# Gate and branch projections of a decoder block turned token-major: h and y as the stationary operand, weights moving in 512 columns

## The reference, cut to what matters

```python
h = rms_norm(x, norm_pre_w)
proj = einsum('bsd,df->bsf', h, w_in)
qkv_a, z_a, beta_a, dec_a, qkv_b, z_b, gate_logits = split(proj, cuts)
...                                                  # mixers: ya, yb, each (1, 256, 1024)
gates = sigmoid(gate_logits + b_gate).reshape(bsz, s, 2, d)
pa = einsum('bsf,fd->bsd', ya, w_branch[0])
pb = einsum('bsf,fd->bsd', yb, w_branch[1])
merged = gates[:, :, 0] * pa + gates[:, :, 1] * pb
out = einsum('bsd,de->bse', merged, w_out)
return x + rms_norm(out, norm_post_w)
```

## Time and profile before

| | us |
|---|---|
| median of 3 runs | 367.78 |
| the profiled execution | 368.02 |
| its span in the trace | 366.2 |
| TensorE busy | 356.7 (97%) |
| VectorE busy | 268.8 (73%) |
| ScalarE busy | 219.8 (60%) |
| GpSimd busy | 59.6 (16%) |

### The profile page before, as it was taken

How to read it: one execution, slowest core, us unless ns; L and a number is a source line. 1 busy time by engine, 2 the same in 40 slices (tenths; PEclk the granted TensorE clock), 3 DMA queues, 4 the chain that set the end, 5 groups by cost and what they waited for, 6 DMA issues and landing times.

```text
span 366.2 us, 7651 instructions
## 1 busy us (share of the span) xinstructions
PE 356.7 (97%) x2755; PEld 343.1 (94%) x2755; DVE 268.8 (73%) x559; ACT 219.8 (60%) x500; POOL 59.6 (16%) x119
## 2 busy tenths in 40 slices
PE   7999998999999999999999999999999999999993
PEld 5889997999999999999999999999999999999882
DVE  2869776488986878978788678797885656767644
ACT  4778894454456565767576676766677542433521
POOL 1533441740033001101020202001020100000011
PEclk9999999999999999999999999999999999999998
DMA  8657849789798475445654455554556484874623
GB/s 261 178 179 196 266 124 236 185 221 242 185 225 225 115 194 150 117 117 130 181 146 120 118 143 152 142 140 117 125 153 181 118 223 127 224 230 170 236 110 115
DMA packets 99343, 62.45 MB, mean 171 GB/s; under 512 B 3652, under 2 KB 94190, under 8 KB 99310
## 3 DMA queue, kind: packets, MB, share of 16 engines
q1 hardware_dynamic: 98014, 58.59, 58.2%
q0 software_dynamic: 1296, 3.43, 3.4%
HBM read 60.41 MB, written 1.59 MB: 169 GB/s over the span
## 4 chain that ended last, share of the span: by engine, by line
PE 92%; DVE 2%; ACT 2%; DMA 1%; issue 1%; POOL 0%; DVEq 0%; SPq 0%; ACTq 0%; POOLq 0%
PE banks L1285 67%; PE banks L1499 6%; PE banks L1303 4%; DMA xin<-in_x_dram 1%; PE banks L1382 1%; PE banks L1389 1%; PE banks L1400 1%; PE banks L1270 1%; DVE w_lo L865 1%; PE banks L1438 1%; PE banks L1202 1%; PE banks L1441 1%; DVE acc L939 1%; PE banks L1227 1%; PE banks L1359 0%
## 5 line engine op out<-in xcount | busy, mean ns | idle before, releaser
L865 DVE TENSOR_TENSOR w_lo<-raw,w_hi 128x1024 fp32r<-128x1024 f32 x102 | 124.2, 1220 | 31.3 <-ACT w_hi L634 31.1
L634 ACT CAST w_hi<-raw 128x1024 fp32r<-128x1024 f32 x103 | 106.8, 1046 | 6.0 <-PE banks L1499 2.8
L1285 PE MATMUL banks<-h_hi,w_lo 128*128 128x256 f32 x568 | 82.3, 287 | 0.0
L1285 PE MATMUL banks<-h_lo,w_hi 128*128 128x256 f32 x568 | 82.2, 287 | 0.0
L1285 PE MATMUL banks<-h_hi,w_hi 128*128 128x256 f32 x568 | 82.2, 287 | 0.0
L1285 PEld LDWEIGHTS banks<-h_hi,w_hi 128*128 128x128 f32 x568 | 72.9, 191 | 0.3
L1285 PEld LDWEIGHTS banks<-h_lo,w_hi 128*128 128x128 f32 x568 | 72.7, 191 | 0.0
L1285 PEld LDWEIGHTS banks<-h_hi,w_lo 128*128 128x128 f32 x568 | 72.7, 191 | 0.0
L939 DVE SCALAR_TENSOR_TENSOR acc<-banks,vec,acc 128x255 f32<-128x255 f32 (+2 forms) x72 | 34.5, 479 | 5.9 <-ACT acc L734 3.5
L584 POOL TENSOR_TENSOR so<-so,rnq 128x2 f32<-128x2 f32 x8 | 3.8, 472 | 148.8 <-ACT junk L801 148.8
L845 ACT CAST h_hi<-tacc 128x256 f32 x8 | 3.3, 408 | 28.4 <-DVE tacc L1166 28.4
(11 more groups left out here) (243 smaller groups left out, 544.4 us busy)
## 6 DMA issues: line engine op xcount, KB each, us to landing
raw<-in_w_in_dram SPq DMA_DIRECT2D x80, 512.0 KB, 5.2
raw<-in_w_branch_dram SPq DMA_DIRECT2D x16, 512.0 KB, 4.8
raw<-in_w_out_dram SPq DMA_DIRECT2D x8, 512.0 KB, 4.2
xin<-in_x_dram SPq DMA_DIRECT2D x2, 512.0 KB, 4.0
th_E<-g_rows POOLq DMA_DIRECT2D x2, 512.0 KB, 6.9
bias<-bias_rows POOLq DMA_DIRECT2D x1, 1024.0 KB, 6.5
raw<-in_x_dram SPq DMA_DIRECT2D x2, 512.0 KB, 4.0
out_dram<-xin SPq DMA_DIRECT2D x4, 256.0 KB, 2.0
```

Source lines behind the costliest of these rows:

```text
L634: nc.scalar.copy(w_hi[:, t % SLOTS, :], raw[:, t % SLOTS, :]).then_inc(s_hi, 1)
L865: v.tensor_tensor(w_lo[:, t % SLOTS, cols], raw[:, t % SLOTS, cols], w_hi[:, t % SLOTS, cols].bitcast(F32), ALU.subtract).then_inc(s_lo, 1)
L1285: last = mm(ps, w, r, start=part == 0 and k == 0, stop=part == 2 and k == KT - 1)
```

## The change

- Gates: four tiles now make a group of 512 gate columns for all 256 tokens, in two banks. The loads take 256 rows x 512 columns (pieces of 2 KB; before 1024 rows x 128 columns, pieces of 512 B). A tile is 12 matmuls of 512 columns (`group_third`). Groups 0 to 2 are tiles 16 to 27, group 3 is tiles 76 to 79.
- The gate bias now lies along the free dimension. ScalarE copies each bank to SBUF (two copies of 128x512 per group), GpSimd adds the bias rows (`gate_rows`, two adds of 128x512 per group, both inputs in SBUF), ScalarE takes the tanh of 128x1024 later (S=66, 78, 122). For group 3 VectorE adds from PSUM (`late_gates`, at S=240), with the tanh at S=243.
- The bias rows are broadcast to 128 partitions by DMA: three on SyncE behind the load of tile 12, one on GpSimd ahead of its last `o_norm`. The b_gate load at the start and one VectorE instruction (`vec_half`) are gone.
- On GpSimd `gate_rows(0)` and `(1)` stand behind the bias DMA (L564) and ahead of the wait for the substitution; `gate_rows(2)` stands between the store and the reload of the solved blocks.
- Branches: no loop. Four groups of four tiles: b and a for columns 0 to 511, then b and a for 512 to 1023. VectorE gates them in tiles of 128x512 and adds them to `m_tok`.
- m is now token-major, and w_out needs it channel-major: TensorE turns it (`turn_m`), 8 transposes of 128x128 at S=270 (tile 90) and 8 behind the second tile of w_out. ScalarE and VectorE split it out of PSUM in pieces of 128x512.

```diff
+GATE_TANH = [66, 78, 122, 3 * BRANCH0 + 3]
+M_TURN = 3 * BRANCH0 + 30
...
+        gate_banks = [(bank[0], bank[1]), (bE, bF), (bA, bD), (bC, bD)]
+        m_banks = [(bA, bB), (bank[0], bank[1])]
...
+                if n == 12:
+                    sp.wait_ge(s_bd_p, 1)
+                    for group in range(3):
+                        part = b_gate[512 * group:512 * group + 512].rearrange("(a n) -> a n", a=1)
+                        sp.dma_start(early_rows[group], part.to_broadcast([P, 512])).then_inc(s_rows_e, 16)
...
+            def gate_rows(group):
+
+                pool.wait_ge(s_rows_e, 48)
+                for c in range(NC):
+                    pool.wait_ge(s_gate_raw, 2 * group + c + 1)
+                    pool.tensor_tensor(th[group][:, c, :], th[group][:, c, :], early_rows[group],
+                                       ALU.add).then_inc(s_gate_b, 1)
+
+            gate_rows(0)
+            gate_rows(1)
             pool.wait_ge(s_sub, 2 * STEPS)
             for a in range(2):
                 pool.dma_start(bass.AP(t_blocks.tensor, BLK * a, [[BLK * BLK, HALF], [2 * BLK, BLK // 2], [1, BLK]]),
                                t0[HALF * a:HALF * a + HALF]).then_inc(s_T_out, 16)
+            gate_rows(2)
             pool.wait_ge(s_T_out, 32)
...
+            def gate_front(group, c):
+
+                if c == 0:
+                    sa.wait_ge(s_gate_p, group + 1)
+                else:
+                    sa.wait_ge(s_tile, GATES_A + 4 * group + 4)
+                nc.scalar.copy(th[group][:, c, :], gate_banks[group][c]).then_inc(s_gate_raw, 1)
+
+            def gate_tanh(group):
+
+                sa.wait_ge(s_gate_b, 2 * group + 2)
+                ac(th[group], th[group], ACT.Tanh, scale=0.5).then_inc(s_gate_th, 1)
...
+            def first_branch(half):
+
+                for c in range(NC):
+                    branch_done(half, 1, c)
+                    v.scalar_tensor_tensor(out=th[half][:, c, :], in0=th[half][:, c, :], scalar=1.0, in1=bank[6 + c],
+                                           op0=ALU.add, op1=ALU.mult).then_inc(s_m_a, 1)
+                    ve.wait_ge(s_m_a, 2 * half + c + 1)
+                    ve.wait_ge(s_m_b, 2 * half + c + 1)
+                    v.tensor_tensor(m_tok[c], m_tok[c], th[half][:, c, :], ALU.add).then_inc(s_m_sum, 1)
...
+            def group_third(n, part, left_hi, left_lo, banks, done):
...
+                for kk in range(2):
+                    for c in range(NC):
+                        left = (left_lo if part == 1 else left_hi)[:, 2 * q + kk, P * c:P * c + P]
+                        right = (w_lo if part == 2 else w_hi)[:, slot, 512 * kk:512 * kk + 512]
+                        last = mm(banks[c], left, right, start=q == 0 and kk == 0 and part == 0,
+                                  stop=q == 3 and kk == 1 and part == 2)
...
+            def turn_m(half):
+
+                pe.wait_ge(s_m_sum, 2 * half + 2)
+                if half == 0:
+                    pe.wait_ge(s_gate_b, 8)
+                for k in range(4):
+                    for c in range(NC):
+                        last = tp(m_banks[half][k // 2][:, SEQ * (k % 2) + P * c:SEQ * (k % 2) + P * c + P],
+                                  m_tok[c][:, P * k:P * k + P], ident)
+                last.then_inc(s_m_turned, 1)
```

More of the change, by code:

```diff
@@ L418, in _ @@
             for g in range(EARLY, 2 * KT):
[L419 to L423, removed]
+                gate_load(GATES_B + g - EARLY, g // 4, g % 4)
+            for t in range(2 * KT):
+                half, branch, q = t // 8, 1 - t // 4 % 2, t % 4
+                group_load(BRANCH0 + t, w_branch[branch][256 * q:256 * q + 256, 512 * half:512 * half + 512])
             sp.wait_ge(s_pv_p, HEADS)
@@ L708, in value_front, with m_parts @@
                                ((bE, bF), (bB, bE))[group][c]).then_inc(s_vtok, 1)
[L710 to L717, removed]
+            def gate_front(group, c):
[7 more added lines that the diff above has]
+                ac(th[group], th[group], ACT.Tanh, scale=0.5).then_inc(s_gate_th, 1)
+            def m_parts(half, b):
+                sa.wait_ge(s_m_turned, half + 1)
+                k = 4 * half + 2 * b
+                nc.scalar.copy(m_hi[:, k:k + 2, :], m_banks[half][b].rearrange("p (k n) -> p k n", k=2)).then_inc(s_m_hi, 1)
             def front(h, s):
@@ L809, in stage_w @@
                     nc.scalar.copy(y_hi[:, 0, g:g + 1, :], one(y32[:, 0, :])).then_inc(s_yhi_a, 1)
-            for S in range(3 * BRANCH0):
+            for S in range(3 * OUT0):
                 n, part = S // 3, S % 3
@@ L829, in _ @@
                         front(g, S - A0 - A_STRIDE * g)
[L830 to L833, removed]
+                for group in range(3):
+                    done = 3 * (GATES_A + 4 * group + 4)
+                    if S in (done, done + 1):
+                        gate_front(group, S - done)
+                    if S == GATE_TANH[group]:
+                        gate_tanh(group)
+                if S == GATE_TANH[3]:
+                    gate_tanh(3)
+                if S in (M_TURN + 1, M_TURN + 2):
+                    m_parts(0, S - M_TURN - 1)
                 if part == 1:
                     split_hi(n + LEAD, n + LEAD, (n + LEAD) // SLOTS + 1)
[L836 to L845, removed]
             for k in range(KT - LEAD):
                 split_hi(OUT0 + k + LEAD, k + LEAD, (OUT0 + k + LEAD) // SLOTS + 1)
+                if k == 2:
+                    for b in range(2):
+                        m_parts(1, b)
             for b in range(2 * NC):
@@ L1018, in front @@
                     ve.wait_ge(s_tanh, HEADS + h + 1)
+                    if h == 0:
+                        ve.wait_ge(s_gate_b, 4)
                     if h >= 2:
@@ new lines, in gate_third @@
+            def gate_third(n, part):
+                group = (n - GATES_A) // 4 if n < HEAD0 else 3
+                if part == 0 and n % 4 == 0:
+                    if group == 0:
+                        pe.wait_ge(s_tap, 3 * HEADS)
+                    elif group == 1:
+                        pe.wait_ge(s_vtok, 4)
+                    elif group == 2:
+                        pe.wait_ge(s_la, 2 * HEADS)
+                        pe.wait_ge(s_k0, HEADS)
+                    else:
+                        pe.wait_ge(s_sc, 2 * HEADS)
+                        pe.wait_ge(s_u, 6 * HEADS)
+                group_third(n, part, h_hi, h_lo, gate_banks[group], s_gate_p)
@@ new lines, in branch_third @@
+            def branch_third(n, part):
+                group = (n - BRANCH0) // 4
+                branch = 1 - group % 2
+                if part == 0 and n % 4 == 0:
+                    if group == 0:
+                        pe.wait_ge(s_gz, 2 * HEADS)
+                        pe.wait_ge(s_ylo_b, HEADS)
+                    elif group == 1:
+                        pe.wait_ge(s_ylo_a, HEADS)
+                    elif group == 2:
+                        pe.wait_ge(s_m_b, 2)
+                    else:
+                        pe.wait_ge(s_m_a, 2)
+                group_third(n, part, y_hi[:, branch], y_lo[:, branch], (bank[6:8], bank[0:2])[branch], s_branch_p)
@@ L1463, in stage_w @@
                     last.then_inc(s_ot_p, 1)
-            for S in range(3 * BRANCH0):
+            for S in range(3 * OUT0):
                 n, part = S // 3, S % 3
                 gates(S)
+                if S == M_TURN:
+                    turn_m(0)
                 if S in TOKENS:
@@ L1511, in _ @@
                 last.then_inc(s_tile, 1)
+                if k == 1:
+                    turn_m(1)
             for c in range(NC):
```

151 lines of the change are left out of this document (94 added, 57 removed).

## The result

The changed kernel takes **369.98 us** (median of 20 runs, 369.27 to 372.12) against 367.88 us of the kernel before beside it: ratio 1.0055, interval 1.0045 to 1.0065. That is 0.55% slower, 2.5 us above the forecast of 367.5 and 0.4 us outside the range. The profiled execution took 369.27 us, its span 367.5.

What follows compares the result with a forecast made beforehand. TensorE, busy for 97% of the span, was taken as the bound. TensorE's -3.16, plus 2.5 for the first four adds' wait and 0.5 for the last pair, gave -0.2 us from 367.78, rounded down to 367.5; range 364.7 to 369.6.

Steps and rivals of the forecast that it cites:

- The matmuls: TensorE's gate and branch tiles: 12 matmuls of 512 columns replace 24 of 256, -4.93 us together.
- the transposes: TensorE, `turn_m`: 16 added transposes at 0.11 us each, +1.77 us, hidden by nothing.
- c: VectorE time lost to the four adds of groups 0 and 1: 4 x 0.75 = 3.0 us, less 0.5 slack.
- d: Cost of `gate_rows(2)`, expected behind the store at about 106 us beside a `w_lo`: 0.5 us, between 0 and 1.3.
- I price no change of it: TensorE's clock: at full level, 2.4 GHz, in every window, so no cost or gain was counted.
- The loads: Larger pieces, same bytes, and row broadcasts between the loads of tiles 12 and 13: nothing, 0.5 us either way.
- the slack of VectorE: First head's convolution before tile 30: could end at 104.3 us, tile 30 due at 104.85, so 0.5 us.
- -3.16: Sum for TensorE alone, matmuls saved and transposes added: -4.93 + 1.77 us.
- faster by more: Whole kernel faster by more than about 0.2% (0.74 us): chance given as 0.37.
- Rival 2: VectorE, slowed by full-length adds, bounds the stretch: +2.8 us, 370.6, or 369.2 with half; slower had chance 0.24.
- point of decision: Whole kernel slower by over 0.74 us when c + d exceeds 4.4 us, faster by as much under 2.9.
- Rival 3: Gate matmuls of 512 columns do not reach 0.2271 us: 367.8 + 1.8 us, chance 2%.

Runs made afterwards that it cites:

- i2: changed kernel with GpSimd adds of one column and 64 B of unused room ahead of h_hi (h at 128 modulo 256): 366.60 us, ratio 0.9960.
- h4: kernel before with 192 B of unused room ahead of h_hi (h at 64 modulo 256), nothing else: 361.07 us, ratio 0.9811.
- e1: changed kernel with all six GpSimd adds on one column instead of 512, other columns' bias left out: 363.80 us, ratio 0.9891.
- p3: changed kernel with 64 B of unused room ahead of h_hi (h at 128 modulo 256, as before): 372.90 us, ratio 1.0127.
- e2: changed kernel with only the last pair of adds moved, behind the reload of the solved blocks and both compactions: 366.13 us, ratio 0.9952.
- g1: changed kernel with the adds of groups 0 and 1 on one column, group 2's pair whole: 367.84 us, ratio 0.9987.
- g2: changed kernel with group 2's second add moved behind the wait for the store's landing, ahead of the reload: 368.93 us, ratio 1.0025.
- e5: complete changed kernel with the six adds behind the first three heads' norms, bias rows loaded per group, tanh later: 365.00 us, ratio 0.9921.
- r1: changed kernel once more, unaltered, a single execution: 370.57 us.
- h3: changed kernel with a GpSimd memset of 128x64 between its wait for the substitution and its store: 370.64 us, ratio 1.0055.
- i1: changed kernel with a GpSimd memset of 128x512 ahead of its store: 369.52 us, ratio 1.0035.

## Why the prediction was wrong, point by point

**The matmuls (-4.93) and the transposes (+1.77): right at the old place, not at the new one.** i2 measured -4.86 and +1.7 at 120 and 227.1 ns. But the prediction priced a matmul as if it were fixed by its shape, and the change moved h. At the new place the fair base is h4: a branch tile costs 24 x 0.1133 = 2.72 us channel-major and 12 x 0.2289 = 2.75 token-major. From tile 16 to 28 e1 gains 0.96 us on h4, and over the 16 branch tiles it loses 0.45; with the 1.7 of the turns TensorE's work is a loss there. The overall result hides this, because the same move made the 1320 remaining channel-major matmuls faster. Against h4 the change costs 8.9 us: 6.2 for the adds (the changed kernel against e1), and 2.7 of e1 against h4, of which the starts of tiles give 1.3 to TensorE's own work (-0.96 + 0.03 for the late gates + 0.45 + 1.74 for the turns) and 1.4 to the stretch from tile 28 to 32. How much of this the move of h gave back depends on the path: 6.9 us by the kernel before and h4 (8.9 - 6.9 = 2.0), 2.9 by p3 and the changed kernel, with a change that costs 5.0 at the old place (5.0 - 2.9 = 2.1). Both end near the measured 2.1.

**The first two pairs of adds (c = 3.0): right.** 2.9 us in the trace. The wait they cause, c - 0.5 = 2.5, was measured as 2.3 (e2 against e1); in the traces e2 is 0.7 us behind e1 at tile 28 and 1.9 at tile 30, where it waits for 1.4.

**`gate_rows(2)` (d = 0.5, between 0 and 1.3): the failed step.** It costs 3.85 us (e2), 4.0 alone (g1). I put the pair at about 106 us, beside the `w_lo` behind the convolution of tile 28, and bounded its price by the length of one add. In fact the first add started at 104.67 us, two adds stood in the queue, the subtraction was shut out through both (g2: 3.3 us for one, 4.5 for two), and it was the one ahead of that convolution, so there was no slack behind it. The other part is the clock, 1.5 us in the profiled execution and more in others: "I price no change of it" was true of the stage as it was, and false behind a wait that the change makes.

**The loads (nothing, 0.5 either way) and the slack of VectorE: wrong, and hidden.** I let TensorE arrive 1.85 us earlier at tile 30 and counted 0.5 us of slack at the convolution only. The same VectorE stretch also releases the loads. i2 lost 1.9 us between tiles 28 and 32, so with adds of one column the early gates brought nothing at the old place: the -3.16 became -1.4 (366.60 against 368.00).

**The rest: right.** No wait at `turn_m`, none for the late gates, none for ScalarE's copies (0.59 us each). The end of the convolution without the adds was reckoned as 104.3 us; e1's is at 104.4. Small slips changed nothing: the earlier trace rows at 289.81 us begins 0.25 us inside tile 79, c + d = 2.5 gives 366.6 and not 366.9, and the chance of "faster by more" adds up to 0.39, not 0.37.

**The rivals.** Rival 2 named the mechanism and the side, and its point of decision, c + d over 4.4, was met by 2.9 + 3.85. But it put 4.7 us on the first two pairs (measured 2.3) and 1.3 on the third (3.85). Its figure, 370.6, is 0.6 us off, with 1.5 us of clock and 6.9 of placement in it that it did not know: the agreement is partly luck. Rival 3 (matmuls that miss 0.2271) had 2%; it came true in part, 0.0018 us per matmul, for a reason that I had not thought of, and its mirror image, a faster 256-column matmul, was not among the cases at all.

The Trainium skill ("SBUF — State Buffer", section "Who interferes with whom") lets the first to issue block the other for the whole instruction. The first two pairs agree: VectorE's products of two SBUF tensors lost 0.7 and 1.1 us and a `w_lo` 1.1, each beside an add of 1.3. The third does not by the starts in the trace: the `w_lo` started 0.85 us ahead of the add and still ended behind both. The measurement decides; the rule gives too little there.

The Trainium skill ("TensorE: Matmul & The Clock Gate", section "What's actually happening") gives 1.2 GHz after idle time. The 213 ns behind 4.5 and 3.0 us agree. Behind 1.4 us of idle time (e2) the matmuls stayed at 113 to 118, so not every idle time does it.

## What to carry to other kernels

Before costing a change of matmul shape, look at whether it moves the operands: a buffer that shrinks by some bytes can outweigh the change, and a control with the old addresses, or the old kernel with the new ones, is the fair comparison. GpSimd work with SBUF operands should not be queued in pairs beside a VectorE instruction that others wait for; behind the last dependent one it was free of that wait (e2, e5). And where one engine's stretch also releases the loads, a gain of TensorE ahead of it is worth only the slack of that stretch.

## What the runs showed of the hardware

The spacing of float32 matmuls of 256 columns was 120.0, 117.8, 116.7 or 113.3 ns, and that of 512 columns 227.1, 228.9 or 232.3 to 233.5 ns, depending on where h and the tensors behind it lie (at one place, that of h4, 117.8 in the gates that read h and 113.3 in the branches that read y); shifts that differ by a multiple of 256 B gave the same numbers (-576 and +192, -512 and 0). Which of the moved tensors counts was not tried. A VectorE subtraction can be held up by two queued GpSimd adds for 3.3 us though its recorded start is 0.85 us ahead of theirs. TensorE's clock fell to 1.2 GHz behind waits of 3.0 us (g1; by their mean clock eight of its ten runs), 3.3 (g2) and 4.4 to 4.7 (changed, r1, h3, i1, p3), not behind one of 1.4 (e2). The lower level held for about 3.4 us in some of these profiles (granted clock 0.86 from 108 to 120 us in the changed kernel) and about twice that in others (0.72 in r1 and h3).
